# A hybrid MLA/Mamba-2/PEER decoder step on one core: two narrow projection slices put in one chunk, and silu of z moved to the projection's drain

## Chip, cores and metric

One core of one Trainium2 chip runs the whole step. The metric is the device time of one launch in microseconds (us), the median of several runs. TensorE is written PE, VectorE DVE, ScalarE ACT, GpSimd POOL, SyncE SP.

## What is computed

The reference is one layer for 512 prompt tokens and 8 sample tokens (520 columns in this kernel, which keeps activations transposed: channels on the partitions, tokens in the columns). What matters here is the input projection and who uses its parts:

```python
h = rms_norm(x, lp['g_mix']) * (1 + sc1) + sh1
proj = h @ lp['w_in']
q_raw, ckv_raw, kpe_raw, z, xbc_raw, dt_raw, gate_a, gate_b = jnp.split(proj, IN_OFFSETS, axis=-1)
kpe = rope(kpe_raw, positions)                       # 64 channels, the key part all heads share
dt = jax.nn.softplus(dt_raw + dt_bias)               # 32 channels, one for each SSM head
y, h_fin = ssd_scan(xs, dt, a, bm, cm, ssm_state)    # xs, bm, cm: convolution and silu of xbc_raw
y = rms_norm(y * jax.nn.silu(z), g_ssm)              # z: 2048 channels
```

Behind it stand the attention over the latents, the gated merge of the two branches, and the expert mixer with 16 of 16384 experts for each of 8 heads, which takes the larger part of the time.

## The kernel before

**Stages.** The kernel is a sequence of blocks; at the end of each block all engines meet at a barrier. In the order of time they are: `conditioned` (norm and modulation of the input), `convolution`, `sample_scan`, `prompt_scan`, `gated_norm`, `attention`, `merge`, `experts`. In each block every engine has its own list of instructions, written by hand, and runs it in order; waits between engines are on semaphores.

**The projection.** It is cut into 74 chunks of 128 output channels, in an order that `projection_columns` (L956) gives: 24 chunks of xbc, one at dt's columns, one at kpe's columns (these 26 are multiplied in `convolution`), then 16 of q and ckv and 16 of z (`sample_scan`), then 16 of gates (`prompt_scan`). The chunks of dt and kpe load 128 columns each, though 32 and 64 are used. `ProjectionWeights` (L357) carries a chunk: SP loads it (L372, 512 KB, two buffers; the load of chunk c waits until chunk c-2 has been split), POOL rounds it to the high part (L379, four buffers, waits for the product of chunk c-4), DVE makes the low part (L346), and PE multiplies 48 matmuls of 260 columns (L352 to L354: 8 slices of the contraction, 2 halves of the tokens, 3 products of high and low parts). Two pairs of PSUM banks take turns, so that the product of chunk c waits for the drain of chunk c-2.

**`convolution`** (L963). For each xbc chunk ACT drains PSUM to `raw` (L1040), starts the sum of the four taps (L1042, L1044), DVE adds three taps (L1081, L1083), and ACT applies silu (L1048). After each product PE transposes eleven rows of the chunk before (L1018, `turn_rows`), and after every fourth chunk DVE copies them out (L1092) and ACT issues two stores (L1054, L1055). After the last xbc chunk ACT's list goes on: the last two of these stores, the drain of dt (L1058), the drain of kpe (L1060); SP then stores kpe to the DRAM scratch `proj[C_KPE]` (L989) and waits for it, and the block ends. POOL fills the matrix `spread` (L997 to L1003) between rounding chunk 25 and chunk 26. DVE splits chunk c+3 at the head of its turn for chunk c.

**`sample_scan`** (L1330). PE multiplies the 32 chunks of q, ckv and z; for each ACT drains PSUM with a copy (L1394) and stores it to `proj` (L1396). Beside it DVE computes dt's softplus and the scan of the 8 sample tokens. ACT's functions other than copies here are an exp, abs and exp at the start (L1385 to L1389) and a small exp after the fourth drain (L1399). **`prompt_scan`** (L1097) begins on ACT with copies (L1241) and then uses exp (L1244 and on).

**`gated_norm`** (L1526). SP loads the 16 chunks of z back from `proj` (L1547) into 7 buffers. For chunk k ACT applies silu in place (L1560), DVE multiplies it into y (L1583), ACT squares the product (L1565) into one of 3 buffers, PE sums the squares over the partitions with a matrix of ones (L1574). In ACT's list the silu of chunk k stands ahead of the square of chunk k-1. At the end ACT takes the root (L1567), DVE the reciprocal (L1585). POOL meanwhile issues the loads of the attention's latents and weights (L447 to L479), and SP, behind the z loads, those of the queries (L461 to L467).

Of the kernel before, what the change touches and what calls it, by code (L numbers as in the profile page):

```python
# [356 lines left out]
class ProjectionWeights:  # L357
# [3 lines left out]
    def __init__(self, nc, n, A, columns):  # L361
        self.view, self.columns = A["w_in"].rearrange("l (k p) n -> p (l k) n", p=P), columns
        self.w, self.hi, self.lo = n.sb("w", [P, 2, KD, P]), n.sb("w_hi", [P, 4, KD, P], F32R), n.sb("w_lo", [P, 4, KD, P], F32R)
        self.w_in = [n.sem(f"w_in{b}") for b in range(2)]
        self.rounded, self.lowered, self.multiplied = (n.sem(k) for k in ("rounded", "lowered", "multiplied"))

    def load(self, sp, first, end):
        for c in range(first, min(end, len(self.columns))):
            if c >= 2:
                sp.wait_ge(self.lowered, c - 1)  # L370
            at = self.columns[c]
            sp.dma_start(self.w[:, c % 2], self.view[:, :, at:at + P]).then_inc(self.w_in[c % 2], 16)  # L372

    def round(self, pool, c):
        if c < len(self.columns):
            pool.wait_ge(self.w_in[c % 2], 16 * (c // 2 + 1))
            if c >= 4:
                pool.wait_ge(self.multiplied, c - 3)
            pool.tensor_copy(self.hi[:, c % 4], self.w[:, c % 2]).then_inc(self.rounded, 1)  # L379
# [576 lines left out]
def projection_columns():  # L956

    at_kpe, at_xbc, at_dt = H * DQK + LAT, IN - 2 * D - SH - CD, IN - 2 * D - SH
    parts_ = (chunks_from(at_xbc, KC) + [at_dt, at_kpe], chunks_from(0, C_KPE) + chunks_from(H * DQK + LAT + ROPE, KI), chunks_from(IN - 2 * D, 2 * D // P))
    return [at for part in parts_ for at in part], (0, len(parts_[0]), len(parts_[0]) + len(parts_[1]))  # L960


def convolution(nc, A, K, S, W, FIRST, h_hi, h_lo, proj, outs, held):  # L963
# [3 lines left out]
    with ExitStack() as ctx:  # L967
# [13 lines left out]
        PC = KC // 2  # L981
        LAST_C = FIRST + KC + 2

        @block.sync
        def _(sp):
            W.load(sp, 1, LAST_C + 2)
            sp.dma_start(outs["conv_s"][0, :, 0:CW - 2, :], A["state_conv"][0, :, 1:CW - 1, :]).then_inc(stored, 16)
            sp.wait_ge(drained, KC + 2)
            sp.dma_start(proj[C_KPE], y[:, 0, :]).then_inc(stored, 16)  # L989
            sp.wait_ge(stored, 32)  # L990
# [17 lines left out]
        def _(pe):  # L1008
# [10 lines left out]

            for c in range(KC + 2):  # L1020
                if c >= 2:
                    pe.wait_ge(drained, c - 1)
                W.product(pe, ps[:, c % 2], FIRST + c, h_hi, h_lo)
                if 1 <= c <= KC:
                    turn_rows(c - 1)

        @block.scalar
        def _(act):
# [29 lines left out]
            act.activation(S["dt_raw"][:, :].rearrange("p (s t) -> p s t", s=2), ps[0:SH, KC % 2, :, 0:HALF], ACT.Copy).then_inc(drained, 1)  # L1058
            act.wait_ge(W.multiplied, LAST_C)
            act.activation(y[:, 0, :].rearrange("p (s t) -> p s t", s=2), ps[:, (KC + 1) % 2, :, 0:HALF], ACT.Copy).then_inc(drained, 1)  # L1060
            for b in range(2):
# [268 lines left out]
def sample_scan(nc, A, K, S, W, FIRST, h_hi, h_lo, proj, acs_dram, outs):  # L1330
# [7 lines left out]
    with ExitStack() as ctx:  # L1338
# [44 lines left out]
        def _(act):  # L1383
# [6 lines left out]
            for c, chunk in enumerate(CHUNKS):  # L1390
                act.wait_ge(W.multiplied, FIRST + c + 1)
                if c >= 2:
                    act.wait_ge(out_stored[c % 2], 16 * (c // 2))
                act.activation(out[:, c % 2].rearrange("p (s t) -> p s t", s=2), ps[:, c % 2, :, 0:HALF], ACT.Copy).then_inc(drained, 1)  # L1394
# [131 lines left out]
def gated_norm(nc, A, K, S, proj, I):  # L1526


    with ExitStack() as ctx:
# [6 lines left out]
        z_in = [m.sem(f"z_in{b}") for b in range(NB)]  # L1536
        gated, silued, squared, added, rooted, chain = (m.sem(n) for n in ("gated", "silued", "squared", "added", "rooted", "chain"))
        gain_in = m.sem("gain_in")
# [17 lines left out]
        def _(act):  # L1556
            for k in range(KI + 1):
                if k < KI:
                    act.wait_ge(z_in[k % NB], 16 * (k // NB + 1))
                    act.activation(z[:, k % NB, :], z[:, k % NB, :], ACT.Silu).then_inc(silued, 1)  # L1560
                if k:
                    act.wait_ge(gated, k)
                    if k > NS:
                        act.wait_ge(added, k - NS)
                    act.activation(sq[:, (k - 1) % NS, :], S["x"][:, k - 1, :], ACT.Square).then_inc(squared, 1)  # L1565
            act.wait_ge(added, KI)
# [12 lines left out]
        def _(dve):  # L1579
            then = Chain(dve, chain)  # L1580
            for k in range(KI):
                dve.wait_ge(silued, k + 1)
                dve.tensor_tensor(S["x"][:, k, :], S["x"][:, k, :], z[:, k % NB, :], ALU.mult).then_inc(gated, 1)  # L1583
# [1172 lines left out]
```

## Time and profile before

| what | value |
|---|---|
| median of 3 runs | 2867.62 us (2862.69 to 2875.89) |
| the profiled execution, first to last instruction | 2876.5 us |
| `convolution` | 55 to 215 us of the span |
| `sample_scan` | 215 to 441 us |
| `prompt_scan` | 441 to 624 us |
| `gated_norm` | 624.6 to 663.9 us |
| `attention`, `merge` | 664 to 1042 us |
| `experts` | 1042 to 2876 us |

In the rows below times are microseconds from the first instruction, PEld is PE's loading of weights, and the arrow in brackets names what ended an engine's idle time. PEclk is the granted clock of TensorE, 1.00 at 2.4 GHz and 0.50 at 1.2 GHz.

### The profile page before, as it was taken

How to read it: one execution, taken by the hardware profiler on the slowest of the kernel's cores; microseconds unless marked ns; L12 is line 12 of the kernel's file. 1: busy time of each engine (PE TensorE's matmuls, PEld its weight loads, DVE VectorE, ACT ScalarE, POOL GpSimd, SP SyncE). 2: the span in 40 equal slices, each digit the busy share in tenths (PEclk: the TensorE clock that was granted, in tenths of full speed). 3: DMA queues.
4: the chain of work that ended last, by engine and by line, in shares of the span. 5: the costliest groups of instructions: out<-in, count | busy, mean ns of one | idle time of the engine just before them, and what ended most of it. 6: DMA issues, size and time to landing. Idle time of an engine off the chain costs nothing.

```text
span 2876.5 us, 36363 instructions
## 1 busy us (share of the span) xinstructions
PE 2433.7 (85%) x11529; PEld 1646.0 (57%) x11529; DVE 2059.7 (72%) x4017; ACT 916.1 (32%) x3611; POOL 1410.3 (49%) x1184
## 2 busy tenths in 40 slices
PE   5999997968989986887999999989989989983353
PEld 3999997854456643444656556655655556552120
DVE  4665887955531118897887888887887879887687
ACT  3431003234330002213444444534444435440110
POOL 1121331210000005776767677767876667776575
PEclk8999998989999998998999999999999999995576
DMA  6324765544025558999989999898989899989997
GB/s 197 91 80 144 216 205 150 136 124 120 11 89 177 177 188 293 401 388 385 348 291 375 348 352 376 307 366 290 400 306 370 293 376 364 347 319 358 401 347 300
DMA packets 375326, 777.12 MB, mean 270 GB/s; under 512 B 46577, under 2 KB 181538, under 8 KB 375097
## 3 DMA queue, kind: packets, MB, share of 16 engines
q0 software_dynamic: 155568, 566.17, 52.7%
q1 hardware_dynamic: 198442, 183.99, 20.2%
q10 hardware_dynamic: 21124, 24.63, 2.6%
q8 instruction: 92, 1.51, 0.2%
q14 instruction: 100, 0.82, 0.1%
HBM read 745.38 MB, written 29.50 MB: 269 GB/s over the span
## 4 chain that ended last, share of the span: by engine, by line
PE 27%; issue 9%; another core or an unknown queue 9%; DMA 6%; DVE 4%; SPq 3%; POOL 2%; ACT 1%; POOLq 0%; DVEq 0%; ACTq 0%
PE mix_pair L2125 19%; DMA mix_u<-in_peer_u,mix_ids 5%; PE mix_pair L2048 2%; DVE mix_acc L2508 2%; PE mix_pair L2140 2%; POOL mix_v L2038 1%; DVE mix_u L2608 1%; SPq L1988 1%; PE mix_pair L2109 1%; DMA pag_kpe<-in_cache_kpe 1%; SPq L1987 1%; PE mix_pair L2127 1%; POOL mix_u L2031 1%; PE mix_pair L2077 1%
## 5 line engine op out<-in xcount | busy, mean ns | idle before, releaser
L2125 PE MATMUL mix_pair<-pag_wx,pag_ckvT 128*128 128x384 f32 (+3 forms) x3072 | 980.7, 467 | 39.4 <-issue 31.3
L2125 PEld LDWEIGHTS mix_pair<-pag_wx,pag_ckvT 128*128 128x128 f32 x3072 | 571.6, 194 | 336.1 <-issue 66.2
L2038 POOL DMA_INDIRECT mix_v<-in_peer_v,mix_ids x512 | 643.5, 1257 | 234.2 <-issue 171.0
L2031 POOL DMA_INDIRECT mix_u<-in_peer_u,mix_ids x512 | 595.6, 1163 | 316.7 <-issue 141.0
L2608 DVE CUSTOM_DVE_ANT_0 mix_u<-mix_u,mix_h 128x1024 f32<-128x1024 f32 x512 | 622.5, 1216 | 172.0 <-DMA mix_u<-in_peer_u,mix_ids 155.1
L2508 DVE SCALAR_TENSOR_TENSOR mix_acc<-mix_v,mix_coef,mix_acc 128x1024 f32<-128x1024 f32 x452 | 577.9, 1278 | 0.0
L2332 ACT ACTIVATE mix_pair<-mix_pair 128x128 f32<-128x128 f32 x1024 | 269.6, 263 | 445.3 <-PE mix_pair L2125 259.1
L379 POOL CAST inp_w_hi<-inp_w 128x1024 fp32r<-128x1024 f32 x74 | 112.2, 1517 | 377.1 <-DMA inp_w<-in_w_in 286.3
L2332 ACT ACTIVATION_READ_ACCUMULATOR mix_pair<-mix_pair 128x1 f32 x1024 | 191.7, 187 | 0.0
L2014 POOL IOTA mix_count_i<- 128x16 int32 x1 | 0.1, 134 | 376.2 <-POOLq L88 376.2
L2140 PE MATMUL mix_pair<-mix_v,mix_diag 128*128 128x512 f32 x224 | 116.5, 646 | 62.8 <-ACT mix_diag L2349 35.1
L352 PE MATMUL stp_ps<-inp_h_hi,inp_w_hi 128*128 128x260 f32 x512 | 148.0, 289 | 13.6 <-DVE inp_w_lo L346 10.4
L354 PE MATMUL stp_ps<-inp_h_hi,inp_w_lo 128*128 128x260 f32 x512 | 146.4, 286 | 0.0
L353 PE MATMUL stp_ps<-inp_h_lo,inp_w_hi 128*128 128x260 f32 x512 | 146.1, 285 | 0.0
L1677 DVE TENSOR_TENSOR mrg_gate<-mrg_psB,mrg_gate 128x520 f32<-128x520 f32 x8 | 5.6, 699 | 184.8 <-PE mrg_psB L1638 184.8
L2320 ACT ACTIVATE pag_ckvT<-mix_pair 128x512 f32<-128x512 f32 x128 | 75.6, 591 | 169.3 <-DMA scn_ce<-keep_acs 68.5
L2341 ACT ACTIVATE mix_coef<-mix_dots 128x4 f32<-128x4 f32 x128 | 25.9, 202 | 306.5 <-DVE mix_dots L2608 279.9
L352 PE MATMUL cnv_ps<-inp_h_hi,inp_w_hi 128*128 128x260 f32 x416 | 120.8, 290 | 0.0
L354 PE MATMUL cnv_ps<-inp_h_hi,inp_w_lo 128*128 128x260 f32 x416 | 118.4, 285 | 0.0
L353 PE MATMUL cnv_ps<-inp_h_lo,inp_w_hi 128*128 128x260 f32 x416 | 118.3, 284 | 0.0
L2077 PE MATMUL mix_pair<-chs_h2T,chs_wq 128*128 128x512 f32 (+2 forms) x352 | 115.9, 488 | 0.9 <-ACT chs_h2T L2304 0.6
L1638 PE MATMUL mrg_psB<-frt_x,mrg_wb 128*128 128x260 f32 x512 | 114.3, 384 | 0.0
(520 smaller groups left out, 4092.1 us busy)
## 6 DMA issues: line engine op xcount, KB each, us to landing
inp_w<-in_w_in SPq DMA_DIRECT2D x74, 512.0 KB, 4.2
pag_ckv<-in_cache_ckv SPq DMA_DIRECT2D x88, 256.0 KB
mrg_w_ada<-in_w_ada SPq DMA_DIRECT2D x8, 2048.0 KB, 9.9
chs_wq<-in_peer_wq SPq DMA_DIRECT2D x11, 1024.0 KB, 16.5
all_shared<-in_cache_ckv SPq DMA_DIRECT2D x40, 256.0 KB
keep_proj<-stp_out ACTq DMA_DIRECT2D x32, 260.0 KB
ada_w_ada<-in_w_ada SPq DMA_DIRECT2D x4, 2048.0 KB, 12.8
stp_st<-in_state_ssm POOLq DMA_DIRECT2D x8, 1024.0 KB, 6.9
```

Source lines behind the costliest of these rows:

```text
L352: pe.matmul(out, w_hi, x_hi, start=first, stop=False)
L353: pe.matmul(out, w_hi, x_lo, start=False, stop=False)
L354: return pe.matmul(out, w_lo, x_hi, start=False, stop=last)
L1638: last = pe.matmul(psB[:, b, s, 0:HALF], wb[:, b, k, :], yT[:, k, s * HALF:(s + 1) * HALF], start=(k == 0), stop=(k == KI - 1))
L2031: pool.indirect_dma_start(u[:, x % UR, :], None, u_rows, bass.IndirectOffsetOnAxis(at, 0)).then_inc(u_in[x % UR], 16)
L2038: pool.indirect_dma_start(v[:, y % VR, :], None, v_rows, bass.IndirectOffsetOnAxis(at, 0)).then_inc(v_in[y % VR], 16)
L2077: last = pe.matmul(bank[2 + side][:, 0:w], wq[:, n % 2, k, side * P:(side + 1) * P], h2T[:, k, cols], start=(k == 0), stop=(k == KD - 1))
L2125: last = pe.matmul(to, ckvT[:, g % 2, k, :], wx[:, k, lo:hi], start=(k == 0), stop=(k == KL - 1))
L2140: last = pe.matmul(psV[:, c, :], diag[:, d % 2, :], v[:, r, c * 512:(c + 1) * 512], start=(x == first_on_pe[t]), stop=(x == last_on_pe[t]))
L2332: last = act.activation(psN[j][:, at:at + NOPE], psN[j][:, at:at + NOPE], ACT.Square, accum_out=ss[:, b % 2, t, h:h + 1])
L2508: dve.scalar_tensor_tensor(acc[:, :], v[:, r, :], c, acc[:, :], ALU.mult, ALU.add).then_inc(v_used[r], 1)
L2608: dve.tensor_tensor_reduce(u[:, r, :], u[:, r, :], h2[:, t % 2, :], 1.0, 0.0, ALU.mult, ALU.add, dots[:, t % 2, slot:slot + 1]).then_inc(u ...
```

## The change

Two edits. First, dt's and kpe's columns form one chunk: its weights are loaded by two transfers of 64 columns (on a semaphore of their own), dt's product comes out on partitions 0 to 31 and kpe's on partitions 64 to 127, and both are drained from the same PSUM pair. `convolution` has 25 chunks instead of 26 and the projection 73 instead of 74; the later blocks keep their chunks, each with an index one lower. Second, the drain of a z chunk in `sample_scan` is a silu instead of a copy, so that `proj` holds silu(z); `gated_norm` multiplies straight from the loaded chunk, and ACT there only squares and takes the root.

```diff
@@ ProjectionWeights
+            if isinstance(at, tuple):
+                for j in range(2):
+                    sp.dma_start(self.w[:, c % 2, :, j * ROPE:(j + 1) * ROPE], self.view[:, :, at[j]:at[j] + ROPE]).then_inc(self.halves_in, 16)
+            else:
+                sp.dma_start(self.w[:, c % 2], self.view[:, :, at:at + P]).then_inc(self.w_in[c % 2], 16)
...
-            pool.wait_ge(self.w_in[c % 2], 16 * (c // 2 + 1))
+            if isinstance(self.columns[c], tuple):
+                pool.wait_ge(self.halves_in, 32)
+            else:
+                pool.wait_ge(self.w_in[c % 2], 16 * sum(not isinstance(at, tuple) for at in self.columns[c % 2:c + 1:2]))
@@ projection_columns
-    parts_ = (chunks_from(at_xbc, KC) + [at_dt, at_kpe], ...
+    parts_ = (chunks_from(at_xbc, KC) + [(at_dt, at_kpe)], ...
@@ convolution
-        LAST_C = FIRST + KC + 2
+        LAST_C = FIRST + KC + 1
...
-            sp.dma_start(proj[C_KPE], y[:, 0, :]).then_inc(stored, 16)
+            sp.dma_start(proj[C_KPE, 0:ROPE, :], y[ROPE:P, 0, :]).then_inc(stored, 16)
...
-            for c in range(KC + 2):
+            for c in range(KC + 1):
...
-            act.wait_ge(W.multiplied, LAST_C)
-            act.activation(y[:, 0, :].rearrange("p (s t) -> p s t", s=2), ps[:, (KC + 1) % 2, :, 0:HALF], ACT.Copy).then_inc(drained, 1)
+            act.activation(y[ROPE:P, 0, :].rearrange("p (s t) -> p s t", s=2), ps[ROPE:P, KC % 2, :, 0:HALF], ACT.Copy).then_inc(drained, 1)
@@ sample_scan
-                act.activation(out[:, c % 2]..., ps[:, c % 2, :, 0:HALF], ACT.Copy).then_inc(drained, 1)
+                act.activation(out[:, c % 2]..., ps[:, c % 2, :, 0:HALF], ACT.Copy if chunk < C_Z else ACT.Silu).then_inc(drained, 1)
@@ gated_norm, ACT
-            for k in range(KI + 1):
-                if k < KI:
-                    act.wait_ge(z_in[k % NB], 16 * (k // NB + 1))
-                    act.activation(z[:, k % NB, :], z[:, k % NB, :], ACT.Silu).then_inc(silued, 1)
-                if k:
-                    act.wait_ge(gated, k)
-                    if k > NS:
-                        act.wait_ge(added, k - NS)
-                    act.activation(sq[:, (k - 1) % NS, :], S["x"][:, k - 1, :], ACT.Square).then_inc(squared, 1)
+            for k in range(KI):
+                act.wait_ge(gated, k + 1)
+                if k >= NS:
+                    act.wait_ge(added, k - NS + 1)
+                act.activation(sq[:, k % NS, :], S["x"][:, k, :], ACT.Square).then_inc(squared, 1)
@@ gated_norm, DVE
-                dve.wait_ge(silued, k + 1)
+                dve.wait_ge(z_in[k % NB], 16 * (k // NB + 1))
```

## Rows read from the trace of the kernel before

**Rows 1.** The page, part 1: busy time and share of the span.
```profile
PE 2433.7 (85%) x11529; PEld 1646.0 (57%) x11529; DVE 2059.7 (72%) x4017; ACT 916.1 (32%) x3611; POOL 1410.3 (49%) x1184
```
**Rows 2.** Windows: us, busy by engine, PEclk, DMA share, GB/s; `experts`.
```profile
1045.00:2876.00 1831.00, 1504.81 (x5566) 904.20 (x5566) 1480.13 (x2952) 661.56 (x3162) 1256.90 (x1041) 0.90 0.93 348
```
**Rows 3.** Timeline of ACT, end of `convolution`: start, duration, instruction, idle before.
```profile
207.04 0.25 ACTq L1054 DMA_DIRECT2D out_conv_p<-cnv_rows_out  x1
207.33 0.29 ACTq L1055 DMA_DIRECT2D out_conv_s<-cnv_rows_out  x1
208.00 0.59 ACT L1058 ACTIVATE stx_dt_raw<-cnv_ps 32x520 f32<-32x520 f32 x1 [1.65 <-DVE cnv_rows_out L1092]
212.07 0.60 ACT L1060 ACTIVATE cnv_y<-cnv_ps 128x520 f32<-128x520 f32 x1 [3.48 <-PE cnv_ps L354]
```
**Rows 4.** Timeline of SP, same place and the start of `sample_scan`.
```profile
212.70 0.36 SPq L989 DMA_DIRECT2D keep_proj<-cnv_y  x1
215.16 0.34 SPq L1377 DMA_DIRECT2D stp_bias<-in_dt_bias  x1
```
**Rows 5.** Windows of 1 us, columns as in rows 2, around that barrier.
```profile
212.00:213.00 1.00, 0.03 (x1) 0.00 (x0) 0.00 (x0) 0.60 (x1) 0.00 (x0) 1.00 0.00 0
216.00:217.00 1.00, 1.00 (x9) 1.00 (x8) 0.00 (x0) 0.46 (x1) 0.00 (x0) 0.72 0.05 0
219.00:220.00 1.00, 1.00 (x7) 1.00 (x6) 0.44 (x2) 0.49 (x1) 0.00 (x0) 0.57 1.16 328
```
**Rows 6.** The same windows around the barrier from `sample_scan` to `prompt_scan`.
```profile
435.00:436.00 1.00, 0.05 (x1) 0.00 (x0) 1.00 (x1) 0.60 (x1) 0.00 (x0) 1.00 0.72 214
438.00:439.00 1.00, 0.00 (x0) 0.00 (x0) 0.00 (x0) 0.00 (x0) 1.00 (x1) 0.66 0.00 0
441.00:442.00 1.00, 0.82 (x4) 0.85 (x5) 0.00 (x0) 0.00 (x0) 0.00 (x0) 0.50 0.00 0
445.00:446.00 1.00, 1.00 (x11) 1.00 (x10) 0.00 (x0) 0.95 (x2) 0.00 (x0) 0.93 0.76 162
```
**Rows 7.** Line L372, loads issued from 176 to 179 us: that of chunk 24.
```profile
L372 SPq DMA_DIRECT2D inp_w<-in_w_in x1: 368/368/368, 176.8 to 176.8; - x1
DMA to landing us min/median/max: 3.7/3.7/3.7
```
**Rows 8.** Timeline, POOL's rounding and DVE's splitting of chunk 24.
```profile
182.94 1.04 POOL L379 CAST inp_w_hi<-inp_w 128x1024 fp32r<-128x1024 f32 x1 [4.81 <-PE cnv_ps L354]
187.62 1.22 DVE L346 TENSOR_TENSOR inp_w_lo<-inp_w,inp_w_hi 128x1024 fp32r<-128x1024 f32 x1
```
**Rows 9.** Waits in `sample_scan`: us in total, times, longest.
```profile
ACT stp_out L1394 <- PE stp_ps L354: 196.3, 32, 12.1
```
**Rows 10.** Timeline of ACT: a table load, a drain, the first copy of `prompt_scan`.
```profile
215.17 1.28 ACT L1385 ACT_TABLE_LOAD   x1 [2.50 <-PEq L967]
245.74 0.60 ACT L1394 ACTIVATE stp_out<-stp_ps 128x520 f32<-128x520 f32 x1 [5.13 <-PE stp_ps L354]
442.30 0.60 ACT L1241 ACTIVATE scn_x_tok<-scn_bank 128x512 f32<-128x512 f32 x1 [6.61 <-PE scn_bank L1186]
```
**Rows 11.** Timeline of ACT in `gated_norm`.
```profile
645.32 0.64 ACT L1560 ACTIVATE mla_k_n<-mla_k_n 128x520 f32<-128x520 f32 x1 [1.48 <-DMA mla_k_n<-keep_proj]
647.35 0.64 ACT L1560 ACTIVATE mla_k_n<-mla_k_n 128x520 f32<-128x520 f32 x1 [0.87 <-DMA mla_k_n<-keep_proj]
648.55 0.64 ACT L1560 ACTIVATE mla_k_n<-mla_k_n 128x520 f32<-128x520 f32 x1
657.33 0.64 ACT L1565 ACTIVATE mla_k_r<-frt_x 128x520 f32<-128x520 f32 x1 [0.24 <-DVE frt_x L1583]
```
**Rows 12.** Timeline of DVE and PE in `gated_norm`; the longest run of sums.
```profile
656.59 0.70 DVE L1583 TENSOR_TENSOR frt_x<-frt_x,mla_k_n 128x520 f32<-128x520 f32 x1 [0.35 <-ACT mla_k_n L1560]
646.54 12.62 PE L1574 MATMUL gtn_ps<-mla_k_r,all_ones 128*128 128x260 f32 x44 [1.50 <-ACT mla_k_r L1565]
```
**Rows 13.** Windows of L1574 alone: us, PE and PEld busy, PEclk, DMA share, GB/s.
```profile
646.00:647.00 1.00, 0.46 (x1) 0.46 (x2) 0.76 1.11 222
649.00:650.00 1.00, 1.00 (x4) 0.75 (x4) 0.53 1.08 403
650.00:653.00 3.00, 3.00 (x15) 2.27 (x13) 1.00 1.00 347
```

More of the change, by code:

```diff
@@ L363, in __init__ @@
         self.w, self.hi, self.lo = n.sb("w", [P, 2, KD, P]), n.sb("w_hi", [P, 4, KD, P], F32R), n.sb("w_lo", [P, 4, KD, P], F32R)
-        self.w_in = [n.sem(f"w_in{b}") for b in range(2)]
+        self.w_in, self.halves_in = [n.sem(f"w_in{b}") for b in range(2)], n.sem("halves_in")
         self.rounded, self.lowered, self.multiplied = (n.sem(k) for k in ("rounded", "lowered", "multiplied"))
@@ L371, in load @@
             at = self.columns[c]
-            sp.dma_start(self.w[:, c % 2], self.view[:, :, at:at + P]).then_inc(self.w_in[c % 2], 16)
+            if isinstance(at, tuple):
[3 more added lines that the diff above has]
+                sp.dma_start(self.w[:, c % 2], self.view[:, :, at:at + P]).then_inc(self.w_in[c % 2], 16)
     def round(self, pool, c):
         if c < len(self.columns):
-            pool.wait_ge(self.w_in[c % 2], 16 * (c // 2 + 1))
+            if isinstance(self.columns[c], tuple):
+                pool.wait_ge(self.halves_in, 32)
+            else:
+                pool.wait_ge(self.w_in[c % 2], 16 * sum(not isinstance(at, tuple) for at in self.columns[c % 2:c + 1:2]))
             if c >= 4:
@@ L958, in projection_columns @@
     at_kpe, at_xbc, at_dt = H * DQK + LAT, IN - 2 * D - SH - CD, IN - 2 * D - SH
-    parts_ = (chunks_from(at_xbc, KC) + [at_dt, at_kpe], chunks_from(0, C_KPE) + chunks_from(H * DQK + LAT + ROPE, KI), chunks_from(IN - 2 * D, 2 * D // P))
+    parts_ = (chunks_from(at_xbc, KC) + [(at_dt, at_kpe)], chunks_from(0, C_KPE) + chunks_from(H * DQK + LAT + ROPE, KI), chunks_from(IN - 2 * D, 2 * D // P))
     return [at for part in parts_ for at in part], (0, len(parts_[0]), len(parts_[0]) + len(parts_[1]))
@@ L1393, in _ @@
                     act.wait_ge(out_stored[c % 2], 16 * (c // 2))
-                act.activation(out[:, c % 2].rearrange("p (s t) -> p s t", s=2), ps[:, c % 2, :, 0:HALF], ACT.Copy).then_inc(drained, 1)
+                act.activation(out[:, c % 2].rearrange("p (s t) -> p s t", s=2), ps[:, c % 2, :, 0:HALF], ACT.Copy if chunk < C_Z else ACT.Silu).then_inc(drained, 1)
                 act.wait_ge(drained, c + 1)
@@ L1536, in gated_norm @@
         z_in = [m.sem(f"z_in{b}") for b in range(NB)]
-        gated, silued, squared, added, rooted, chain = (m.sem(n) for n in ("gated", "silued", "squared", "added", "rooted", "chain"))
+        gated, squared, added, rooted, chain = (m.sem(n) for n in ("gated", "squared", "added", "rooted", "chain"))
         gain_in = m.sem("gain_in")
```

## The prediction

> **What bounds the kernel now.** The first view to read is the busy table: PE is busy for 85% of the span [rows 1]. That share is a mean over eight stages with different limits, so the next view is the stages themselves. `experts` is 1831 us of the 2876.5 and the change touches nothing in it [rows 2]; whatever is gained lies ahead of 664 us. Inside `convolution` and `sample_scan` PE sets the pace: ACT waits 196.3 us for PE's products in `sample_scan`, once for each of its 32 drains [rows 9]. But the barrier that ends a stage is set by whatever comes last on any engine, so for each edit I read the timeline at the end of its stage. In `gated_norm` no engine is busy throughout: up to the chunk that starts at 647.35 ACT waits for z's transfers, and from 648.55 on it doesn't any more [rows 11].
>
> **Part 1, one chunk less in `convolution`.** A chunk is 48 matmuls. The last one of before ends at about 212.0 (the ACT drain behind it starts at 212.07), and the one that goes away takes from about 206.2 to there, some 5.8 us. The saving isn't 5.8 us, because ACT's list is late too. Before, the drain of dt starts at 208.00, behind the issues of two stores at 207.04 and 207.33, while its product had been ready since 206.2; ACT then waits 3.48 us for the kpe product [rows 3]. That wait goes. What comes last now is ACT's own list: dt's drain from 208.00 to 208.59, kpe's drain right behind it. Before, the store of kpe was issued 0.63 us after kpe's drain began (212.70 against 212.07), and the next stage began 2.46 us after that (215.16) [rows 3, 4]. So: 208.59 + 0.63 + 2.46 = 211.68 instead of 215.16, a gain of 3.48 us. The store is now 64 partitions instead of 128; no row has half of this store, so its price lies between nothing and a few tenths of gain, and I take nothing. The least it can bring is little below 3.5, unless dt's drain is later; the most is the full chunk, 5.8, if ACT's two store issues and dt's drain were to move up as well, for which nothing in the change gives a reason.
>
> From this comes a cost. PE stops at 206.3 instead of 212.03 and starts again at 211.7 instead of 215.2: an idle time of 5.4 us instead of 3.2. The granted clock shows what idling does here: after the 3.2 us gap it fell to 0.50 (1.2 GHz) at about 216.3 and was back at about 219.9 (the means of 0.72 and 0.57 in the two windows say where in them it changed), so some 3.5 us of products ran at half speed [rows 5]. At the next barrier PE was idle from 435.05, the clock fell at 438.3, PE resumed in the window from 441 and the clock was back at 445.07, 3.9 us later [rows 6]. With 5.4 us of idling the first stretch will look like that second one: 3.9 us at half instead of 3.5, which costs 0.2 us more. Bounds: nothing, and 1 us if the return took 5.5 us. I take 0.2.
>
> The joint chunk's weights come as two transfers of 256-byte rows instead of one of 512-byte rows. The one load was issued at 176.8 and took 3.7 us to land, to 180.5 [rows 7]; POOL rounds this chunk only at 182.94, after waiting for PE, and DVE splits it at 187.62 [rows 8]. If each half took as long as the whole, one behind the other, it would be there at 184.2, rounded by 185.3, and DVE would still be in time: cost nothing. It would have to take 9.8 us (186.6, plus 1.04 of rounding) to be late for DVE, and then DVE, not PE, would be the first to wait. The Trainium skill bears on this ("DMA: Bandwidth & Descriptors", Specifications): it gives 512 B as the least run for full rate and says that below it the engines read, modify and write. By that rule the load would be longer, by a factor that the page doesn't state; no row of before has this load in runs of 256 B, and the sum doesn't use it. POOL's filling of `spread` moves one chunk earlier, ahead of the rounding of chunk 25 instead of 26; the same work, with the next product 10 us away. The two small drains that were apart on ACT stand together, counted above. Splitting one chunk less on DVE (1.22 us) and rounding one less on POOL (1.04 us) [rows 8] is worth nothing, since neither ends the stage.
>
> **Part 2, silu in the drain.** In `sample_scan` a silu of 128x520 takes the place of a copy: 0.64 [rows 11] against 0.60 us [rows 10], sixteen times, on an engine that idles 5.13 us before such a drain [rows 10]. PE reuses a PSUM pair one chunk later, so the drain has a whole chunk's time; 0.04 us disappears in it. Silu is not in the set of functions that ACT holds here, so one table load comes ahead of the first z drain, and one ahead of the first exp of `prompt_scan`; a table load is 1.28 us [rows 10]. The first lies in the 5.13 us, the second in the 6.61 us before ACT's first copy or the idle time behind the copies. Cost nothing; if both were on the path, 2.6 us. The Trainium skill has a rule against this edit ("ScalarE: Activation LUTs", Table sets: the hidden batching unit): calls should be grouped by set, and here silu goes between two uses of exp. The same page (What ACT_TABLE_LOAD costs) puts a switch at 2.66 us with its drain; by that figure two switches on the path would be 5.3 us. In the trace the row shows 1.28 us for the load, and both places are covered by either figure.
>
> **Part 3, `gated_norm` without silu.** Before, a chunk costs ACT two functions, and from 648.55 on the chunks follow each other by ACT alone (0.62 to 0.64 us each, overlapping a little). Also, in ACT's list square k-1 stands behind silu k, so while transfers are slow every square waits for the next chunk's transfer. The last square starts at 657.33 and PE's sums end at 646.54 + 12.62 = 659.16, that is 1.19 us after that square is done (657.97) [rows 11, 12]. Now the chunk goes from its landing to DVE (0.70), to ACT's square (0.64), with about 0.04 us for each hand-over: PE can begin 1.42 us after the landing. Taking the starts of silu after a DMA wait as landings, PE starts chunk 6 at 645.32 + 1.42 = 646.74 and chunk 7 at 647.35 + 1.42 = 648.77. I leave the landings where they are, as the DMA queues are full (share 1.08 to 1.11) [rows 13]. From chunk 7 on three things could set the pace: DVE at 0.70, ACT at 0.64, PE at its own rate. PE's rate with work waiting is 14 or 15 records in 3 us at full clock, 4 records a chunk, so about 0.86 us [rows 13]. PE is now the slowest: **the limit of the second half of this stage moves from ACT to PE**, and the gain is what PE's rate leaves.
>
> PE's clock counts here. It fell to half at about 646.5 and was back at 649.95 [rows 13]. I assume the same around the same activity, a fall at about 646.8 and a return at 650.2. Chunk 6 then takes 1.72, chunk 7 runs at half from 648.77 to 650.2 (0.72 of its 0.86 done) and ends at 650.34; chunk 15 starts seven chunks later, at 656.36, and with 1.19 us ends at 657.55 instead of 659.16. **Gain 1.6 us.** Bounds: if the clock stays at half until 3.9 us after 648.77, the delay at the other barrier [rows 6], 2.5 us more at half cost 1.25, and the gain is 0.35. If PE caught up at no cost, DVE would set the pace: chunk 7 multiplied at 648.05, chunk 15 at 653.65, squared at 654.3, summed at 655.5, a gain of 3.7. The loads of the queries that SP issues behind z start about that much earlier or at the same time, and nothing at the head of `attention` waits for them.
>
> **The sum.** 3.48 - 0.2 + 1.6 = 4.9 us. Against the profiled execution that is 2876.5 - 4.9 = 2871.6. That execution is 8.9 us longer than the median of the three runs; from the median, 2867.6 - 4.9 gives 2862.7. This is 0.17%. The measurement of this kernel can tell about 0.5% (14.3 us), and the three runs before alone are 13.2 us apart. Forecast: no change that can be measured.
>
> **The rivals.** (a) Both edits bring all that they remove: 5.8 us for the chunk, 3.7 us in `gated_norm`, 9.5 in sum, 2858.1. For it speaks that PE paces `convolution`; against it dt's drain at 208.00, which does not depend on the removed product [rows 3]. (b) Slower by the clock: in `gated_norm` PE's sums come in short bursts, and if the granted clock stayed at half from 648.77 on, nine chunks of 1.72 us would end at 664.25 (plus 0.3 of tail), 5.4 us later than before instead of 1.6 earlier. With part 1's 3.3 that is 2.1 us slower, 2869.7. It decides as soon as the clock is at half for more than about 7 of the 16 us from 648.77 on. Against it: before, the clock came back 3.4 us after it fell while PE was densely busy, and PE will be denser now [rows 13]. (c) The parts are as forecast but `experts` ends elsewhere: its DMA share is 0.93 over 1831 us [rows 2], the gathers there start at another time, and repeats of one and the same kernel already differ by 13.2 us. This moves the result by up to some 9 us to either side, 2854 to 2872, and at times beyond. (d) The change doesn't do what it says, since the stage ends do not depend on the removed work: for part 1 that would need the stores issued at 207.04 and 207.33 to land last; they would have to take over 4 us, while the larger store of kpe takes 2.46 to the next stage's start [rows 3, 4]. Then only 1.6 is left, 2866.
>
> **How the numbers follow.** Forecast 2862.7: 0.67. (a) 0.08, (b) 0.05, (c) beyond the forecast's own few us 0.16, (d) 0.04. The range takes in (a), (b), (d) and most of (c): 2854 to 2872. Beyond 0.5% faster (under 2853.3) lies only a part of (c), 0.05; beyond 0.5% slower (over 2882) 0.02; within 0.5%, 0.93.
>
> **What would show it.** Right: dt's and kpe's drains stand back to back on ACT at 208.0 to 208.6 and `sample_scan` begins near 211.7; table loads appear ahead of the first z drain and at the head of `prompt_scan`, with PE not waiting for either; in `gated_norm` DVE's multiplications wait for DMA alone up to chunk 7, squares wait for DVE, and PE's last sum ends about 1.6 us earlier after the stage's start than before (33 us after SP's first issue there instead of 34.5). Wrong: `sample_scan` starting at 209.4 or 215; ACT's drains of z held by table loads one by one; POOL's rounding of chunk 24 waiting for DMA past 186.6; PE at half clock beyond 653; or a difference of over 5 us in `experts`, which these steps don't treat.

## The result, and the profile after

The changed kernel takes 2857.14 us in the median (2845.36 to 2880.5, 22 runs), the kernel before beside it 2867.33 (2857.6 to 2895.95, 22 runs). The ratio is 0.9947, 95% interval 0.9928 to 0.9966: 13.2 us by the means (9.7 to 20.6 by the interval). The forecast was 2862.7, 4.9 us less, and "no change that can be measured". A second comparison on another chip, in the experiments below, gave 0.9974 (0.996 to 0.9988), 6.8 us by the means. A run over 1.5% above the fastest of its kernel counts as slow and is left out of the means; of the kernels compared below that is one run of att_after (847.6 us). The profiled execution of the changed kernel has a span of 2847.7 us. Page, part 1 and the row of part 3 that will matter; the columns of the first line are as in [rows 1], those of the second are packets, MB and the share of 16 DMA engines:

```profile
PE 2422.3 (85%) x11481; PEld 1640.1 (58%) x11481; DVE 2059.3 (72%) x4016; ACT 910.1 (32%) x3596; POOL 1416.7 (50%) x1183
...
q8 instruction: 92, 1.51, 0.2%
```

48 matmuls and 16 of ACT's functions are gone (one table load has come); so the change removes the work that it says. DVE and POOL have one split and one rounding less.

**The end of `convolution`**, ACT, then SP, to be read against [rows 3, 4]:

```profile
206.37 0.29 ACTq L1062 DMA_DIRECT2D out_conv_s<-cnv_rows_out  x1
207.04 0.59 ACT L1065 ACTIVATE stx_dt_raw<-cnv_ps 32x520 f32<-32x520 f32 x1 [2.43 <-DVE cnv_rows_out L1098]
207.66 0.60 ACT L1066 ACTIVATE cnv_y<-cnv_ps 64x520 f32<-64x520 f32 x1
210.97 1.28 ACT L1391 ACT_TABLE_LOAD   x1 [2.71 <-PEq L974]
...
208.28 0.52 SPq L996 DMA_DIRECT2D keep_proj<-cnv_y  x1
210.95 0.36 SPq L1383 DMA_DIRECT2D stp_bias<-in_dt_bias  x1
```

The 3.48 us wait for the second product is gone, the two drains stand back to back, and the store follows 0.62 us after the second one starts. The whole list lies 0.96 us earlier than in the execution before; that is chance of the earlier stages, so I measure from PE's last transposition of `convolution` to the next stage: 9.13 us before, 5.88 here. With the product removed the stage does end earlier, so rival (d) is out.

**The two loads of the joint chunk** (line L374; issue and landing) and POOL's rounding of that chunk:

```profile
L374 SPq DMA_DIRECT2D inp_w<-in_w_in x2: 368/476/584, 175.9 to 176.3; - x2
DMA to landing us min/median/max: 3.3/3.6/3.9
...
181.98 1.05 POOL L386 CAST inp_w_hi<-inp_w 128x1024 fp32r<-128x1024 f32 x1 [4.80 <-PE cnv_ps L354]
```

The half loads of 256-byte runs took 3.3 and 3.9 us; the last is there at 180.2, and POOL starts after waiting for PE, as in [rows 8]. The whole load took 3.7 [rows 7]. The two lay side by side, and the whole chunk was there 4.3 us after its first issue; 0.4 us of the 0.6 more is the distance of the two issues. The Trainium skill ("DMA: Bandwidth & Descriptors", Specifications) gives 512 B as the least for full rate. This trace bears a slower rate out by 0.2 us at most, for the same 512 KB.

**The clock behind the longer idle time**, windows with columns as in [rows 5]:

```profile
212.00:213.00 1.00, 1.00 (x6) 1.00 (x6) 0.00 (x0) 0.26 (x1) 0.00 (x0) 0.50 0.05 0
214.00:215.00 1.00, 1.00 (x8) 1.00 (x8) 0.00 (x0) 0.97 (x2) 0.00 (x0) 0.69 0.98 276
215.00:216.00 1.00, 1.00 (x11) 1.00 (x10) 0.64 (x2) 0.29 (x1) 0.00 (x0) 1.00 1.17 338
```

PE now resumes at 1.2 GHz and has 2.4 GHz back at about 214.6, some 3.6 us after its first product (211.01).

**The table loads**, ACT ahead of the first z drain and at the head of `prompt_scan`:

```profile
319.64 0.33 ACTq L1402 DMA_DIRECT2D keep_proj<-stp_out  x1
320.05 1.28 ACT L1400 ACT_TABLE_LOAD   x1 [0.44 <-ACT stp_out L1400]
326.37 0.61 ACT L1400 ACTIVATE stp_out<-stp_ps 128x520 f32<-128x520 f32 x1 [5.03 <-PE stp_ps L354]
...
438.17 1.28 ACT L1250 ACT_TABLE_LOAD   x1
440.84 1.06 ACT L1250 ACTIVATE scn_seg<-scn_seg 128x1024 f32<-128x1024 f32 x1 [1.39 <-DVE scn_seg L1284]
```

Behind each load ACT still waits, 5.03 us for PE and 1.39 us for DVE: both loads are hidden, as forecast. The z drain is 0.61 us.

**`gated_norm`**, ACT, then PE, then DVE, then windows with columns as in [rows 5]:

```profile
637.47 0.64 ACT L1567 ACTIVATE mla_k_r<-frt_x 128x520 f32<-128x520 f32 x1 [1.89 <-DVE frt_x L1585]
644.40 0.64 ACT L1567 ACTIVATE mla_k_r<-frt_x 128x520 f32<-128x520 f32 x1 [0.53 <-PE gtn_ps L1576]
647.29 0.64 ACT L1567 ACTIVATE mla_k_r<-frt_x 128x520 f32<-128x520 f32 x1 [0.24 <-PE gtn_ps L1576]
648.16 0.64 ACT L1567 ACTIVATE mla_k_r<-frt_x 128x520 f32<-128x520 f32 x1 [0.24 <-PE gtn_ps L1576]
650.74 0.69 ACT L1569 ACTIVATE mla_y_rstd<-gtn_ps,all_eps 128x520 f32<-128x520 f32 x1 [0.63 <-PE gtn_ps L1576]
...
640.47 10.23 PE L1576 MATMUL gtn_ps<-mla_k_r,all_ones 128*128 128x260 f32 x36 [0.21 <-ACT mla_k_r L1567]
...
641.89 4.65 DVE L1585 TENSOR_TENSOR frt_x<-frt_x,mla_k_n 128x520 f32<-128x520 f32 x7 [0.90 <-DMA mla_k_n<-keep_proj]
...
637.00:638.00 1.00, 0.00 (x0) 0.00 (x0) 0.44 (x1) 0.53 (x1) 0.00 (x0) 0.94 1.12 188
644.00:645.00 1.00, 1.00 (x4) 0.78 (x4) 1.00 (x2) 0.60 (x1) 0.00 (x0) 0.65 1.05 397
```

Squares wait for DVE while transfers are slow, and the last five of the 16 wait for PE, the last two at a pace of 0.87 us (647.29 to 648.16): the limit has moved to PE at the rate that the forecast used (0.86). But the root stands 34.54 us after the stage's first issue (616.20), where it stood 34.63 us after it before. The windows show one reason: the clock was at half from 637.9 to 644.7, 6.8 us, where it was at half for 3.4 us before [rows 13] and the forecast had taken 3.4. Measured from the stage's first issue it came back after 28.5 us, about where the forecast's lower bound had it (652.7, 28.0 us after the start at 624.6 before); that bound was a gain of 0.35 us. One pair of executions can't weigh this term; several are averaged below.

### The profile page after: what moved, and what is told of

Same layout as the page of the kernel before. It is cut to its first block, busy times and chain, and to the rows that moved or that the text cites. A ratio compares the mean times of both kernels' runs of the same rounds, so it can differ in the third digit from the quotient of the medians.

```text
span 2847.7 us, 36248 instructions
## 1 busy us (share of the span) xinstructions
PE 2422.3 (85%) x11481; PEld 1640.1 (58%) x11481; DVE 2059.3 (72%) x4016; ACT 910.1 (32%) x3596; POOL 1416.7 (50%) x1183
## 4 chain that ended last, share of the span: by engine, by line
issue 19%; PE 13%; another core or an unknown queue 10%; DMA 7%; DVE 5%; POOL 5%; SPq 4%; ACT 1%; POOLq 0%; DVEq 0%; ACTq 0%
PE mix_pair L2127 8%; DMA mix_u<-in_peer_u,mix_ids 6%; POOL mix_v L2040 3%; POOL mix_u L2033 2%; DVE mix_acc L2510 2%; PE mix_pair L2050 2%; SPq L1990 2%; DVE mix_u L2610 2%; SPq L1989 1%; SPq L1988 1%; PE mix_pair L2079 1%; DMA pag_kpe<-in_cache_kpe 1%; PE mix_pair L2142 1%; PE mix_pair L2150 1%
## 5 line engine op out<-in xcount | busy, mean ns | idle before, releaser
L2033 POOL DMA_INDIRECT mix_u<-in_peer_u,mix_ids x512 | 614.7, 1201 | 297.1 <-issue 148.9
L2040 POOL DMA_INDIRECT mix_v<-in_peer_v,mix_ids x512 | 628.9, 1228 | 221.7 <-issue 161.9
L2343 ACT ACTIVATE mix_coef<-mix_dots 128x4 f32<-128x4 f32 x128 | 25.9, 202 | 296.7 <-DVE mix_dots L2610 272.8
```

The costliest lines, as they stand in the source:

```text
L2033: pool.indirect_dma_start(u[:, x % UR, :], None, u_rows, bass.IndirectOffsetOnAxis(at, 0)).then_inc(u_in[x % UR], 16)
L2040: pool.indirect_dma_start(v[:, y % VR, :], None, v_rows, bass.IndirectOffsetOnAxis(at, 0)).then_inc(v_in[y % VR], 16)
```

## The experiments

**1. The part ahead of `experts`, and each edit alone.** All four kernels leave out `experts` (two thirds of the time and the noisiest part); front_chunk has the joint chunk alone, front_silu the silu drain and the new `gated_norm` alone.

```diff
-            experts(nc, A, K, L, parts, shared, D_, outs)
+            pass
```

> The kernel of before without its experts stage (y_p and y_s stay unwritten), to time the stages ahead of it by themselves. Both theories expect about 1042 us plus a few, with a spread between executions much smaller than the 38 us that 22 runs of the whole kernel show; if the spread stays at ten or more us, the stages ahead of experts are a source of it.

> The changed kernel without its experts stage (y_p and y_s stay unwritten). Theory A, that the whole gain of 10 to 15 us arises ahead of experts: 10 to 15 us less than the front of before. Theory B, that the stages ahead gain the 4 to 6 us of the sum and the rest arises in experts: 4 to 7 us less.

> The front of before with the joint chunk of dt and kpe alone (no experts stage; y_p and y_s stay unwritten). By the sum, 3.3 us less than the front of before; if the stages behind convolution gain from the shift as the profiles hint (sample_scan 3.2 us shorter), 6 to 8.

> The front of before with silu in the drain alone (no experts stage; y_p and y_s stay unwritten). By the sum, 1.6 us less than the front of before; by the profile after, in which gated_norm is as long as before (39.2 against 39.3 us), nothing.

Medians (means) of 5 runs: 1052.93 (1051.5), 1039.39 (1038.6), 1046.01 (1045.7) and 1049.31 (1048.7). By the means the whole change brings 12.9 us with a standard error of 2.3, the chunk alone 5.9 (2.3), silu alone 2.9 (2.9); from here on a number in brackets behind a gain is its standard error. So the gain arises ahead of `experts`. The chunk alone has a gain clear of noise, silu alone has not, and the errors are too large to divide the 12.9 between them. The profiles show where: the stretch from PE's last transposition to `sample_scan` is 5.90 us in front_chunk and 9.14 in front_silu, nearly the forecast's difference. A second place was not: from the last z drain to `prompt_scan` it is 5.58 us in front_before and 5.62 in front_silu, but 4.76 in front_after and front_chunk.

**2. How far the gain has come at two earlier ends.** The scan kernels leave out `gated_norm`, `attention`, `merge` and `experts`; the att kernels leave out `merge` and `experts`.

```diff
-                gated_norm(nc, A, K, S, D_["proj"], I)
-                attention(nc, A, K, L, I, oT, S["x"][:, KI:KC, :], outs, S["x"][:, 0:KI, :], S["g_ssm"])
+                pass
+                pass
```

> The kernel of before cut behind prompt_scan (gated_norm, attention, merge and experts left out), some 626 us. Its partner below tells where ahead of 1042 us the 13 us of difference between the two fronts arise.

> The changed kernel cut behind prompt_scan. By the terms that the traces show apart from the clock (3.2 us at the end of convolution, about 1 at the end of sample_scan): 4 to 5 us less than its partner. If the rest of the 13 us is TensorE's clock and arises in these stages: 8 to 12 less. If it arises in gated_norm and attention: 4 to 5.

> The kernel of before cut behind attention (merge and experts left out), some 840 us.

> The changed kernel cut behind attention. With its partner: 13 us less, if the difference is all there by then; by the terms apart from the clock (3.2, 1, and 0.9 in gated_norm) 5 us. The two profiles also give each stage's share of half clock once more.

Up to the end of `prompt_scan`: means 629.2 and 621.9, a gain of 7.3 (1.3), between what I expected without a part of the clock (4 to 5) and with one (8 to 12). Up to the end of `attention`: 844.5 and 837.1, a gain of 7.4 (3.0), where I expected 5 or 13. The runs of att_after fall in groups, 834.4 to 834.9 with a mean granted clock of 0.949 in all three, and 844.4 with 0.929: runs of one and the same kernel differ by 10 us, and their clock with them.

**3. The clock.** The pair again, and the pair with PE's idle places filled with products of a constant that nobody reads, 128x128 each, at the ends of the stages ahead of `attention` and around the sums of `gated_norm` (22 of them at the end of `prompt_scan`, for example; in three places the changed kernel has another number of them, since its gaps differ):

```diff
+            pe.wait_ge(drained, GATES)
+            warm(pe, K, ps[:, 0, 0, 0:P], 22)
```

> The front of before once more (experts left out, y_p and y_s unwritten), for a second profile and five more times. Theory C, that the change brings some 6 to 7 us by its own steps and what was measured beyond it is chance of TensorE's granted clock: 1044 to 1056 us, whatever the mean clock.

> The changed front once more (experts left out, y_p and y_s unwritten). Theory C: 6 to 8 us less than its partner, once both are put to the same granted clock. Theory D, that the change makes the clock itself better: 11 to 15 us less, with a mean clock 0.003 or more higher again.

> The front of before with idle time of TensorE filled by products that nobody reads (128x128, at the ends of conditioned, convolution, sample_scan, prompt_scan and gated_norm and between the first sums of gated_norm); experts left out. If half clock behind barriers costs what the rows show, some 5 to 10 us less than the front without them.

> The same filling in the changed front (experts left out). With the clock's part taken out, the difference to its partner is what the change's own steps bring. Theory C: 5 to 8 us less than the filled front of before. Theory D: under 5, since the clock's part is gone from both.

Means: 1049.0 and 1040.2 without the filling, a gain of 8.8 (1.3); with it, 1042.9 and 1035.1, a gain of 7.8 (2.0). The first lies between what I expected without an effect of the clock (6 to 8) and with one (11 to 15), the second within what I expected without one (5 to 8). Weighted by their errors, the three pairs without `experts` give **9.3 us (1.0)**, which excludes the 4.9 of the sum. In each of these three pairs the changed kernel also has the higher mean granted clock (0.9504 against 0.9452, 0.9512 against 0.9464, 0.9727 against 0.9684). The filling itself gains 6.1 us (1.8) on the kernel before and 5.1 (1.5) on the changed one. An estimate of the clock's part: the time lost to the clock (span times one minus the clock) is 57.6 us before and 51.5 after in the first pair, 56.2 and 50.8 in the second, 33.0 and 28.3 in the filled one. Between runs of one kernel, all kernels pooled, a microsecond lost goes with some 0.5 us of the run's time (single kernels, with five runs each, scatter widely around it). By that 2.3 to 3 of the 9.3 us go with the clock. This is a correlation and not shown as a cause. The chunk alone doesn't have it: front_chunk gained 5.9 us with a mean clock of 0.9438, below the 0.9452 of front_before. Why the changed kernel should have a higher clock the runs don't show.

**4. What ends `sample_scan`, whether PE bounds `gated_norm`, and the whole kernels.** front_swap lets chunk c of the weights land in the other of the two buffers; front_half_sums leaves out half of the sums of squares.

```diff
-            sp.dma_start(self.w[:, c % 2], self.view[:, :, at:at + P]).then_inc(self.w_in[c % 2], 16)
+            sp.dma_start(self.w[:, (c + 1) % 2], self.view[:, :, at:at + P]).then_inc(self.w_in[c % 2], 16)
```

```diff
-                for s in range(2):
+                for s in range(2 if k in (0, KI - 1) else 1):
```

> The kernel before without its experts stage, and with one edit: the two buffers that the projection weights alternate between change places (chunk c lands in buffer (c + 1) % 2 instead of c % 2; same transfers, same order). It asks why sample_scan ends earlier behind its last z drain where the joint chunk is made. The profiles so far have 5.5 to 6.1 us from that drain to the next stage without the joint chunk (mean 5.75) and 4.6 to 4.8 with it (mean 4.70); the last thing to finish is a weight chunk, which is the 59th with two chunks for dt and kpe and the 58th with one, so it lies in the other buffer. Theory B (the buffer's address sets how long the landing takes): 4.6 to 4.8 us here, with the load landing 7.7 us after its issue instead of 9.0. Theory N (it is not the buffer, but what runs beside the transfer): 5.5 to 6.1 us as before. All else, the end of the convolution (9.13 us) and gated_norm (40.0) among it, is as before under both.

> The changed kernel without its experts stage, and with half of the sums of squares in gated_norm left out: the second half of the columns is summed for the first and the last chunk only, so PE has about half the work per chunk there. It asks whether PE is the new limit of that stage, as I forecast. If it is (theory A): from the ninth or so chunk on squares no longer wait for PE (before the edit each waits 0.24 to 0.53 us), the pace is DVE's 0.70 us a chunk, the square root comes 32 to 33 us after the stage's first load issue instead of 34.5, and the stage takes 36.5 to 37.8 us instead of 38.9 (mean of the changed form). If the transfers set the pace and the waits for PE are slack (theory D): root at 34 to 34.5 us, and the stage at 38.4 to 39.

> The whole changed kernel with PE kept busy over its idle places: some 16 to 54 small products of a constant at the ends of the stages ahead of attention, into PSUM that nobody reads. On the kernels without experts this filling brought 6.1 us on the kernel before and 5.1 on the changed one, and the granted clock over the span rose from 0.946 to 0.968. Here, if experts is left as it is: 4 to 6 us below the changed kernel (chance of experts ending elsewhere: some 9 us either way), so a ratio to the kernel before of 0.992 to 0.994. If the filling's gain is lost in experts (its DMA phase absorbs it): equal to the changed kernel.

> The changed kernel, whole and as it is, once more beside the kernel before on this chip. If what the runs without experts showed carries through it (9.3 us with an uncertainty of 1), its ratio is 0.9968 with the interval's half width of some 0.003. If experts adds to the gain (13 us and more, as the first comparison read), 0.9955 or less.

front_swap: 5.64 us from the last z drain to the next stage. It isn't the buffer. What it is can be read in the view of DMA traffic over the transfer of that last weight chunk; rows: queue, packets, MB, share of 16 engines; then the load, KB, us from issue to landing. The kernel before, 428 to 438 us, and the 1 us window from 434:

```profile
q8 instruction: 1, 0.02, 0.6%
inp_w<-in_w_in SPq DMA_DIRECT2D x1, 512.0 KB, 9.0
...
q8 instruction: 1, 0.02, 5.5%
```

The changed kernel, 422 to 431 us:

```profile
out_ssm_s<-stp_st POOLq DMA_DIRECT2D x1, 1024.0 KB, 8.0
inp_w<-in_w_in SPq DMA_DIRECT2D x1, 512.0 KB, 7.7
```

Before, one piece of instructions (0.02 MB) is fetched in the middle of the transfer; it takes 5.5% of 16 engines in 1 us, that is 0.88 us of one engine, and the load lands 1.3 us later than in the changed kernel, which has no such row there. I take the queue for PE's code: 92 pieces of 16.4 KB stand to 11481 matmuls, one for 125, and of the kernel without `experts` there were 47 pieces before and 50 with the filling's 322 more matmuls. The joint chunk takes 48 matmuls out of the code, so all later pieces are fetched at another point of the work: its kernels without filling have a fetch 3.3 to 4.3 us ahead of the states' store and the next 19 to 21 us behind it, and the transfer lies between. In all seven profiles without the joint chunk and without filling, front_swap among them, the fetch lies 5.4 to 6.8 us behind the issue of the states' store, the load lands 8.4 to 9.0 us after its issue, and POOL's rounding comes 9.3 to 9.9 us behind the store; in all eight with the joint chunk up to here there is no fetch in that time, and these are 7.6 or 7.7 and 8.4 to 8.5. The filled kernels, whose code lies otherwise, tell the fetch from the joint chunk. front_warm_before, 424 to 433 us:

```profile
inp_w<-in_w_in SPq DMA_DIRECT2D x1, 512.0 KB, 7.6
```

front_warm_after, 419 to 430.2 us:

```profile
q8 instruction: 1, 0.02, 0.6%
inp_w<-in_w_in SPq DMA_DIRECT2D x1, 512.0 KB, 9.3
```

Without the joint chunk but with no fetch the load is early (rounding 8.40 us behind the store), with the joint chunk and a fetch it is late (10.10, and 9.82 in warm_full). How one piece does it is not shown: a piece that met the load took 0.88 to 1.00 us, while the load landed 0.8 to 1.7 us later than the mean of those without one (7.6).

front_half_sums, ACT, then windows of 1 us (columns as in [rows 5]):

```profile
647.90 0.64 ACT L1567 ACTIVATE mla_k_r<-frt_x 128x520 f32<-128x520 f32 x1 [0.23 <-PE gtn_ps L1576]
652.05 0.69 ACT L1569 ACTIVATE mla_y_rstd<-gtn_ps,all_eps 128x520 f32<-128x520 f32 x1
...
648.00:649.00 1.00, 1.00 (x4) 0.76 (x3) 0.74 (x2) 0.77 (x2) 0.00 (x0) 0.50 1.05 391
650.00:651.00 1.00, 1.00 (x5) 0.51 (x4) 0.00 (x0) 0.98 (x3) 0.00 (x0) 1.00 1.10 403
```

The root comes 32.14 us after the stage's first issue (619.91), against 33.97 in the mean of the seven profiles with the new form and all sums; the stage takes 36.78 us, the shortest of all. With half of PE's work gone it is 1.8 us earlier, and 0.9 us earlier than in the best of the seven (33.07). It is one execution, but it agrees with the waits of the squares: PE is the limit. Squares still waited for it, since the clock was at half up to 649.3, and there two matmuls take as long as four at full. My statement that they would not wait was wrong.

The whole kernels, 12 runs each beside 23 of before (2804.0 in the median): after_full 2796.47, ratio 0.9974 (0.996 to 0.9988), 6.8 us by the means (1.7); warm_full 2790.72, ratio 0.9961 (0.9944 to 0.9978), 11.3 us (2.0). The gain carries through `experts`, and `experts` adds nothing that these runs can tell: 13.2 (2.9) and 6.8 (1.7) on whole kernels lie around the 9.3 (1.0) of the front. The filled kernel is the fastest of the three, 4.5 us (2.3) below the changed one as I expected (4 to 6); its ratio to the kernel before missed the 0.992 to 0.994 that I had written, since the changed kernel itself had gained less here.

**5. Moving PE's code by products at the start.** 80 products in front_code_before and 48 in front_code_after, in two places, to swap the two positions of the code:

```diff
+            for _ in range(40):
+                pe.matmul(psX[:, 0, 0, 0:1], K["ident"][:, :], K["ident"][:, 0:1], start=True, stop=True)
             pe.wait_ge(cT_ready, 1)
```

> The kernel before without its experts stage, and with 80 products of one column added while PE waits for the first weights of the program (up to 30 us, two places of 40). They compute nothing that is read; they only move all of PE's later code by 80 products, so that it lies against the 16 KB pieces in which it is fetched as the changed kernel's does. Theory C (code): with two chunks for dt and kpe a piece of PE's code (0.02 MB, 0.9 us of one DMA engine) is fetched some 6 us behind the store of the states at sample_scan's end, among the packets of the last weight chunk, which then lands about 1 us later; where no piece falls there, the stage ends earlier. So here: no fetch within 10 us behind that store, 8.4 to 8.5 us from the store's issue to POOL's rounding (9.3 to 9.9 in the seven profiles without the joint chunk), 4.6 to 4.8 us from the last z drain to the next stage (5.5 to 6.1). Theory J (the joint chunk does it in some other way): 9.3 to 9.9 and 5.5 to 6.1 as before. The median: about 1 us below front_before (1052.9 and 1048.9 on two chips), too little to be told.

> The changed kernel without its experts stage, and with 48 products of one column added at the same two places (24 and 24), as many as the joint chunk removes, so that PE's code behind the convolution lies against its 16 KB pieces as in the kernel before. Theory C (code): a fetch some 6 us behind the store of the states, 9.3 to 9.9 us from that store's issue to POOL's rounding (8.4 to 8.5 in the seven profiles with the joint chunk), and 5.5 to 6.1 us from the last z drain to the next stage (4.6 to 4.8). Theory J (the joint chunk itself): 8.4 to 8.5 and 4.6 to 4.8 as in the changed kernel.

Neither did what I wrote. PE in front_code_before, the first place:

```profile
6.28 17.23 PE L240 MATMUL ada_psX<-all_ident 128*128 128x1 f32 x80
```

Each product of this type became two matmuls, so the code moved by twice what I meant, and 80 records took 17.23 us where PE had 6 us to spare: the medians, 1072.03 and 1052.61, are 19 to 23 and 12 to 13 us above the kernels without these products and say nothing about the change. What the runs do show is two more positions of the code. With some 125 matmuls to a piece, a move by 160 should bring the fetch about 35 matmuls earlier than in the kernel before. It was found 4.2 us behind the store instead of 5.4 to 6.8, which is earlier, but by less than 35 matmuls take (some 4.2 us at the 0.12 us of one product at full clock), so the count of matmuls alone doesn't place a fetch. The load landed late (9.3 us after its issue, rounding 10.13 behind the store, 6.34 us from the last drain to the next stage). front_code_after, moved by 96 against the changed kernel, has its fetch 3.4 us ahead of the store and none in the transfer, a landing of 7.7 us and 4.75 us at the end. So in all 20 profiles, ten with a fetch in the transfer and ten without, the late landing and the fetch go together, in both kinds of kernel. The clean test, exchanging the two positions alone, remains undone.

## Why the prediction was wrong

Means over profiles: six or seven executions of the old form of each stage, seven to nine of the new one.

**Part 1, end of `convolution`: right.** Forecast 3.48, measured 3.24 (from PE's last transposition to the next stage 9.12 to 9.14 us in the seven profiles without joint chunk and filling, 5.88 to 5.90 in the eight with it). Of the missing 0.24, 0.21 is the store: 2.67 us from its issue to the next stage, not the 2.46 of the larger one [rows 4]. I had taken that half the partitions could only be cheaper, and they weren't. dt's drain didn't move against the rest of ACT's list, so rival (a)'s 5.8 is out.

**The clock behind it: sign right, size 0.4 instead of 0.2.** From `sample_scan`'s start to its first drain it is 7.60 us in six of the seven profiles without the joint chunk, and 7.69 to 8.18 with it (mean 7.97 of nine). In the seventh, att_before, the clock didn't fall there at all, and it is 6.05 us.

**A term that the sum lacked: 1.0 us at the end of `sample_scan`.** 5.73 us (5.52 to 6.08) from the last z drain to the next stage without the joint chunk, 4.70 (4.61 to 4.76) with it. I costed the removed matmuls by their time alone. They are also some 6 KB of code (an estimate: 48 of 125 matmuls in 16.4 KB), and the end of this stage hangs on a load that a code fetch met before and doesn't meet now. The page has the queue of instructions, and I hadn't asked where its pieces fell.

**Part 2: right.** Both table loads hidden, no wait added; front_silu shows nothing in `sample_scan`.

**Part 3, `gated_norm`: right in mechanism, and in size partly by luck.** Forecast 1.6. The root stands 35.50 us behind the stage's first issue in the mean of the seven profiles of the old form without filling (34.63 to 36.24) and 33.97 in the seven of the new one (33.07 to 34.94): 1.5 us (0.3). The forecast had 33.0 against 34.5, so both of its ends were some 1.0 us early: the profiled execution before happened to be 1.0 us better than the mean of the other six. Two premises failed. DVE waited for transfers up to chunk 9 (0.90 us at 641.89), not up to 7; and the clock's return is not the same in every execution. In the three profiles of the new form where it came 27.8 to 28.7 us behind the stage's first issue the root stands at 34.53 to 34.94, in the four where it had come by 25.9 at 33.07 to 34.15. A good execution before and a late clock in the one after account for the first pair of traces showing nothing.

These terms sum to 3.24 - 0.4 + 1.0 + 1.5 = 5.3 us, close to the forecast's 4.9, which is luck in part: half of the missing 1.0 is made up by the other three terms, which were taken 0.5 too high in all.

**What failed is, first, the step from the sum to the change in time.** The front gained 9.3 (1.0), and about 4 us of it stand in no place that I can name. Most of them are there early: up to the end of `prompt_scan` the gain is 7.3 (1.3), while the terms up to there, 3.24 - 0.4 + 1.0, make 3.8. Of the 4 us, 2.3 to 3 go with a higher mean granted clock over the whole front, which the sum had at -0.2; between 1 and 2 us stay open, and so does why the clock is higher. **Second, the step from the sum to "no change that can be measured".** It took 0.5% (14.3 us) as what a measurement can tell. The interval of the first comparison was 0.19% to either side (5.4 us), that of the second 0.14% (3.9 us), so even the forecast's own 4.9 us was at the edge of being measured, and 9.3 us was beyond it. The stage lengths can't find the missing microseconds: `prompt_scan` is 184.2 us in the mean without the joint chunk (181.8 to 189.2) and 183.4 with it (181.0 to 187.1), and `attention` varies from 174 to 184 with no order.

**The chances.** The range, 2854 to 2872, held the median of the first comparison, and the second comparison's interval (3.4 to 11.2 us) holds the sum. But faster by over 0.5% had 0.05, and the first comparison read 0.53%. With 9.3 us true (0.33%) and an interval of 0.19% to either side, a reading over 0.5% comes in about one case in 25; the second comparison read 0.26%. So that the first one passed 0.5% was partly chance, but of the comparison and not, as I had it, of `experts`. What I should have given a chance to was a gain under 0.5% that is still told from none. Rival (a) had the right size, 9.5 us, for the wrong reasons: neither the chunk nor `gated_norm` brought all that was removed. Rival (b) didn't come, though its sign nearly did: 653 is 28.4 us behind that stage's start before, and in the profile after the clock was at half until 28.5 us behind it (644.7). But (b) needed over 7 us at half from 24.1 us on (648.77 before), and it was 4.4. Rival (c) stays as noise.

## What to carry to other kernels

Where a stage ends at a barrier, follow each engine's list and the last transfer to that barrier: here the forecast of 3.48 us came out as 3.24 and that of 1.6 as 1.5. Removing or adding matmuls also moves the points at which PE's code is fetched, and where a barrier hangs on one transfer, that went with 1 us either way here; look where the instruction queue's packets fall before calling such an edit free. One profiled execution before and one after can't weigh terms of 1 us, since a stage differs by as much between executions; measured on a cut kernel, over several profiles, they can. Before a forecast of "nothing that can be measured", work out the interval from the number of runs: a spread of 13 us between three runs became an interval of 5.4 us with 22.

## What the runs showed of the hardware

A fetch of what I take for PE's code is one packet of 16.4 KB; those beside the last weight load of `sample_scan` took 0.88 to 1.00 us each. That 512 KB load landed after 8.4 to 9.3 us with such a fetch in its time (ten profiles) and after 7.6 to 7.7 without (ten). A table load of ACT took 1.28 us, and the next function could start right behind it (1.29 us from start to start, before: 657.98 to 659.27). Products of one column with full f32 weights came out as two matmuls, 0.215 us a record (17.23 us for 80, front_code_before). Executions of one kernel differed by 10 us together with the mean granted clock, 0.949 or 0.929 (att_after).
